# A decoder block with 64 experts: routing loops written out and reordered, and experts with three buffers for gathered rows and for down weights

## The reference, cut to what matters

```python
merged = jax.nn.sigmoid(gate_c) * y_conv + jax.nn.sigmoid(gate_a) * y_attn
h = h + merged @ w_out[l]                                  # (2064, 1024) @ (1024, 1024)
hn = rmsnorm(h, norm2_g[l])
g_logits = hn @ w_group + b_group                          # 8 groups
g_w, g_idx = max and argmax of softmax(g_logits)
e_logits = (hn @ w_router + b_router)[:, g_idx]            # 8 experts of the chosen group
top_l, top_i = lax.top_k(e_logits, 2)
w = softmax(top_l) * g_w
# each token goes to two of the 64 experts:
hb = jax.nn.silu(xb @ w_gate[e]) * (xb @ w_up[e])          # 1024 -> 256
y = hb @ w_down[e]                                         # 256 -> 1024
h = h + segment_sum(w * y)                                 # then the 16 meta tokens are dropped
```

## Time and profile before

| | |
|---|---|
| time, median of 3 runs | 2815.13 us (2812.27 to 2816.78) |
| the profiled execution's own time, and its span | 2826.66 us, 2825.0 us |
| busy in the span: PE, PEld, DVE, ACT, POOL | 89%, 71%, 62%, 37%, 20% |
| DMA | 477.69 MB, mean 169 GB/s |
| routing, 1690 to 1998 us | PE busy 233.41 of 308 us, granted clock 0.88, DMA share 0.41 |
| start of the experts, 1998 to 2042 us | PE busy 25.70 of 44 us, clock 0.70, DMA share 0.39 |
| jobs in full flow, 2042 to 2715 us | PE busy 626.23 of 673 us, clock 0.99, DMA share 0.90 at 344 GB/s |
| last jobs, 2715 to 2825 us | PE busy 77.75 of 110 us, clock 0.88, DMA share 0.52 |

### The profile page before, as it was taken

The page is one execution under the profiler, slowest core; times in us unless marked ns, Lnnn a source line. Parts: engine busy times, 40 slices in busy tenths (PEclk is TensorE's granted clock), DMA queues, the critical chain, the costliest instruction groups (busy, mean ns, idle before and its releaser), DMA issues. The chain is left out here.

```text
span 2825.0 us, 36971 instructions
## 1 busy us (share of the span) xinstructions
PE 2515.1 (89%) x12303; PEld 2017.3 (71%) x12303; DVE 1755.8 (62%) x2528; ACT 1048.6 (37%) x1524; POOL 566.6 (20%) x502
## 2 busy tenths in 40 slices
PE   4999999999899899999929998886499989999986
PEld 3898888999878798898916776665366666666652
DVE  6599997776120288888835554555466666666641
ACT  4201001443221287787821113222344444444430
POOL 3132222111111011111110010021323333333321
PEclk9999999999999999999969998998699999999998
DMA  5121212233214424345057646334388989899983
GB/s 128 46 67 54 74 52 83 75 113 113 87 65 132 125 81 107 92 126 147 16 150 198 181 142 233 122 134 164 112 342 338 351 333 354 339 342 345 351 314 136
DMA packets 181933, 477.69 MB, mean 169 GB/s; under 512 B 33292, under 2 KB 104076, under 8 KB 147372
## 3 DMA queue, kind: packets, MB, share of 16 engines
q1 hardware_dynamic: 132658, 370.45, 39.0%
q0 software_dynamic: 33264, 58.98, 6.2%
q10 hardware_dynamic: 15890, 46.67, 4.3%
HBM read 415.40 MB, written 117.21 MB: 189 GB/s over the span
## 5 line engine op out<-in xcount | busy, mean ns | idle before, releaser
L92 PE MATMUL project_bank<-project_xnT_hi,project_w_hi 128*128 128x512 f32 (+4 forms) x1352 | 511.2, 378 | 1.3 <-DVE project_xnT_lo L667 0.7
L93 PE MATMUL project_bank<-project_xnT_lo,project_w_hi 128*128 128x512 f32 (+4 forms) x1352 | 498.9, 369 | 0.0
L94 PE MATMUL project_bank<-project_xnT_hi,project_w_lo 128*128 128x512 f32 (+4 forms) x1352 | 496.7, 367 | 0.0
L717 DVE SCALAR_TENSOR_TENSOR project_work<-project_work,project_taps 128x2048 f32<-128x2048 f32 x128 | 335.5, 2621 | 4.5
L2404 DVE TENSOR_TENSOR experts_gu_lo<-weights_gate_up,experts_gu_hi 128x2048 fp32r<-128x2048 f32 x128 | 288.0, 2289 | 62.3 <-ACT experts_gu_hi L2346 61.9
L2346 ACT ACTIVATE experts_gu_hi<-weights_gate_up 128x2048 fp32r<-128x2048 f32 x128 | 244.3, 1911 | 163.7 <-DMA weights_gate_up<-in_w_up_dram 136.6
L2308 PE MATMUL experts_y_bank<-weights_down,experts_hT 128*128 128x512 f32 x544 | 256.9, 616 | 27.3 <-issue 26.3
L92 PEld LDWEIGHTS project_bank<-project_xnT_hi,project_w_hi 128*128 128x128 f32 (+1 forms) x1352 | 251.4, 186 | 36.9 <-issue 8.5
L93 PEld LDWEIGHTS project_bank<-project_xnT_lo,project_w_hi 128*128 128x128 f32 (+1 forms) x1352 | 251.2, 186 | 33.2 <-issue 6.8
L94 PEld LDWEIGHTS project_bank<-project_xnT_hi,project_w_lo 128*128 128x128 f32 (+1 forms) x1352 | 251.5, 186 | 27.2 <-issue 0.6
L1088 DVE TENSOR_TENSOR attend_pT<-attend_t_bank,attend_pT 128x512 fp32r<-128x512 f32 (+3 forms) x352 | 214.2, 615 | 23.7 <-ACT attend_pT L1038 22.7
(11 more groups left out here) (264 smaller groups left out, 4482.9 us busy)
## 6 DMA issues: line engine op xcount, KB each, us to landing
weights_gate_up<-in_w_gate_dram SPq DMA_DIRECT2D x68, 1024.0 KB
weights_gate_up<-in_w_up_dram SPq DMA_DIRECT2D x68, 1024.0 KB
weights_down<-in_w_down_dram SPq DMA_DIRECT2D x68, 1024.0 KB
project_w_raw<-in_w_in_dram SPq DMA_DIRECT2D x36, 512.0 KB, 4.1
qk_d<-project_work SPq DMA_DIRECT2D x16, 1032.0 KB, 5.4
gate_d<-project_work ACTq DMA_DIRECT2D x16, 1024.0 KB, 4.2
merge_gates<-gate_d SPq DMA_DIRECT2D x16, 1024.0 KB, 5.5
first_half<-qk_d SPq DMA_DIRECT2D x24, 512.0 KB, 15.7
```

What stands on the lines that cost most here:

```text
L92: pe.matmul(out, lhs[0], rhs[0], start=first, stop=False)
L93: pe.matmul(out, lhs[0], rhs[1], start=False, stop=False)
L94: return pe.matmul(out, lhs[1], rhs[0], start=False, stop=last)
L717: nc.vector.scalar_tensor_tensor(out=work[:, 2, 0:SEQ], in0=work[:, 1, META - 1 + q:META - 1 + q + SEQ], scalar=taps[:, bass.ds(ct, 1), q] ...
```

## The change

- **Routing.** All loops are written out. The conversion of the merged tile (c, 3) to high and low parts no longer stands in tile (c, 2) but in the tail of the chunk before, on ACT ahead of the two Exp and on DVE inside `choose` behind its eighth step (except in chunk 0). The last tile is turned into a free half of `h_bank` (`turned`) and its turn no longer waits for `lower` of the tile before. In the last chunk the logits are made in two groups of 256 tokens, the first ahead of the last turn; the former first step of `find_slots` is `take_ranks`, and for chunk 2 it runs in the last tile, the rest of `find_slots(2)` behind the last `lower`. The scatters of an expert choice k = 0 start as soon as its slots are there. The jobs are stored by two DMAs in place of four.
- **Experts.** Down weights have three rooms (`room_of`, `uses_of_room`), gathered rows and their indices three buffers (`room`, `times_loaded`, `freed`): `load_down(n)` waits for the down product of job n-3, and rows are gathered three jobs ahead. The third down room is taken from the stage's own memory. The order of the instructions in a step is as before.
- **The start of the experts.** DVE zeroes the three row buffers in place of POOL; POOL zeroes `sofar` behind the first three gathers; SP waits for job 0's rows before it loads the weights of jobs 2 and 3.
- **The first jobs** and SP's loads for them are written out on every engine; the further jobs keep their loops.

The core of the diff (left out: declarations and plain renamings of call arguments):

```diff
@@ -1563,24 +1563,22 @@
-def over_chunks(eng, tile, tail, after):
-    for j in range(CHUNK):
-        tile(0, j)
-        if j:
-            after(0, j - 1)
-    def chunk(c):
+def turned(n):
+    return t_bank if n < NT - 1 else h_bank[:, n % 2 ^ 1]
+def over_chunks(tile, tail, after):
+    for c in range(NC):
...
             tile(c, j)
-            tail(c - 1, j, False)
+            if c:
+                tail(c - 1, j, False)
...
                 after(c, j - 1)
-            tail(c - 1, j, True)
-    with eng.Fori(1, NC - 1) as c:
-        chunk(c)
-    chunk(NC - 1)
+            if c:
+                tail(c - 1, j, True)
@@ -1649,9 +1646,9 @@
 def scatter(c):
-    wait(pool, slots_ready, c * 4 + 4)
-    for j in range(CHUNK):
-        for k in range(2):
+    for k in range(2):
+        wait(pool, slots_ready, c * 4 + (3 + k))
+        for j in range(CHUNK):
@@ -1670,9 +1667,10 @@
 pe.wait_ge(hn_ready, n + 1)
-pe.wait_ge(hn_lo_ready, n + 1)
+if n < NT - 1:
+    pe.wait_ge(hn_lo_ready, n + 1)
 for i in range(DC):
-    m = nc.tensor.transpose(t_bank[:, i // 4, (i % 4) * P:(i % 4 + 1) * P],
+    m = nc.tensor.transpose(turned(n)[:, i // 4, (i % 4) * P:(i % 4 + 1) * P],
@@ -1691,16 +1689,24 @@
+def logits(c, first, end):
+    pe.wait_ge(hn_lo_ready, c * CHUNK + (end + 1))
+    pe.wait_ge(w_ready, DC + 1)
+    cols = slice(first * P, end * P)
+    for i in range(DC):
+        m = pair_matmuls(nc.tensor, r_bank[0:R, cols], (r_hi[:, i, :], r_lo[:, i, :]),
+                         (hnT_hi[:, i, cols], hnT_lo[:, i, cols]), i == 0, i == DC - 1)
+    return m
 def tail(c, part, behind):
+    last = c == NC - 1
     if part == 0 and not behind:
+        if last:
+            pe.wait_ge(slot_step, (c - 1) * 5 + 1)
+            logits(c, 0, CHUNK // 2)
...
     elif part == 1 and not behind:
-        pe.wait_ge(hn_lo_ready, c * CHUNK + (CHUNK + 1))
-        pe.wait_ge(w_ready, DC + 1)
-        for i in range(DC):
-            m = pair_matmuls(nc.tensor, r_bank[0:R, :], (r_hi[:, i, :], r_lo[:, i, :]),
-                             (hnT_hi[:, i, :], hnT_lo[:, i, :]), i == 0, i == DC - 1)
-        m.then_inc(logits_done, 1)
+        logits(c, CHUNK // 2 if last else 0, CHUNK).then_inc(logits_done, 1)
@@ -1773,18 +1780,18 @@
     elif part == 1:
+        if c < NC - 1:
+            high_m(c + 1, CHUNK - 1)
...
-over_chunks(act, tile, tail, high)
+over_chunks(tile, tail, high)
...
 act.dma_start(jobs_d[:, 0:1], job_count[:, :]).then_inc(final_stored, 16)
-for k in range(3):
-    act.dma_start(jobs_d[:, 1 + MORE_JOBS * k:1 + MORE_JOBS * (k + 1)].rearrange("o j -> j o"),
-                  job[:, k:k + 1], allow_slow_non_contiguous=True).then_inc(final_stored, 16)
-wait(act, final_stored, 64)
+act.dma_start(jobs_d[:, 1:1 + 3 * MORE_JOBS].rearrange("o (j k) -> (o j) k", k=3),
+              job[:, 0:3], allow_slow_non_contiguous=True).then_inc(final_stored, 16)
+wait(act, final_stored, 32)
@@ -1811,22 +1818,25 @@
 nc.vector.tensor_tensor(hnT_lo[:, :, j * P:(j + 1) * P],
-                        t_bank[:, :, :].rearrange("p b (c t) -> p (b c) t", t=P),
+                        turned(n)[:, :, :].rearrange("p b (c t) -> p (b c) t", t=P),
...
 s = stat[:, b, :]
-if j < CHUNK - 1:
+if j == CHUNK - 1:
+    if c < NC - 1:
+        low_m(c + 1, 0)
+elif j < CHUNK - 2 or c == 0:
     low_m(c, j + 1)
-elif not (isinstance(c, int) and c == NC - 1):
-    low_m(c + 1, 0)
...
                         x_sb[:, b, :], ALU.add).then_inc(h_ready, 1)
+if n == NT - 1:
+    take_ranks(NC - 2)
@@ -1885,6 +1895,8 @@
 step(v.tensor_reduce(e(2), p64.rearrange("p t (g j) -> p t j g", j=PER_GROUP), AX.X, ALU.add))
+if c < NC - 1:
+    low_m(c + 1, CHUNK - 1)
@@ -1915,12 +1927,14 @@
+def take_ranks(c):
+    wait(dve, rank_done, c + 1)
+    nc.vector.scalar_tensor_tensor(out=place[:, :, :].rearrange("p t n -> p (t n)"),
+                           in0=r_bank[:, 0:CHUNK * EXPERTS], scalar=float(EXPERTS),
+                           in1=index64_tiled[:, :], op0=ALU.mult, op1=ALU.add).then_inc(slot_step, 1)
...
     v = nc.vector
-    wait(dve, rank_done, c + 1)
-    v.scalar_tensor_tensor(out=place[:, :, :].rearrange("p t n -> p (t n)"),
-                           in0=r_bank[:, 0:CHUNK * EXPERTS], scalar=float(EXPERTS),
-                           in1=index64_tiled[:, :], op0=ALU.mult, op1=ALU.add).then_inc(slot_step, 1)
@@ -1938,16 +1952,19 @@
         lower(c, CHUNK - 1)
+        if c == NC - 1:
+            find_slots(c - 1)
...
         choose(c)
-    elif part == 3 and behind:
+    elif part == 3 and behind and c != NC - 2:
+        take_ranks(c)
...
 wait(dve, tiled, CHUNK)
-over_chunks(dve, tile, tail, lower)
+over_chunks(tile, tail, lower)
@@ -1983,6 +2000,16 @@
+def room_of(n):
+    return (n + 1) % 3
+def uses_of_room(n):
+    return sum(room_of(m) == room_of(n) for m in range(n + 1))
@@ -1993,8 +2020,10 @@
+self.down_rooms = {1: self.down[:, 0, :, :], 2: self.down[:, 1, :, :]}
 self.gate_up_loaded = [ctx.enter_context(nc.semaphore(f"weights_gate_up_loaded{b}")) for b in range(2)]
-self.down_loaded = [ctx.enter_context(nc.semaphore(f"weights_down_loaded{b}")) for b in range(2)]
+self.down_loaded = [ctx.enter_context(nc.semaphore(f"weights_down_loaded{b}")) for b in range(3)]
@@ -2082,15 +2113,25 @@
-def over_first_jobs(eng, step):
-    for n in range(4):
-        step(n, n % 2, n // 2, min(n, 3), 2)
-    with eng.Fori(2, EXPERTS // 2 - 1) as q:
-        for b in range(2):
-            step(q * 2 + b, b, q, 3, 2)
-    step(EXPERTS - 2, 0, EXPERTS // 2 - 1, 3, 1)
+def over_first_jobs(step):
+    for n in range(EXPERTS - 1):
+        step(n, n % 2, n // 2, min(n, 3), min(EXPERTS - 1 - n, 3))
+def room(n, b):
+    return room_of(n) if isinstance(n, int) and n < EXPERTS else b
+def times_loaded(n, b, q):
+    if isinstance(n, int) and n < EXPERTS:
+        return uses_of_room(n)
+    return q + (uses_of_room(EXPERTS - 2 + b) + 1 - EXPERTS // 2)
+def freed(n):
+    return n if isinstance(n, int) and n < EXPERTS else n + 1
@@ -2143,16 +2184,17 @@
 def load_down(n, b, e):
-    wait(sp, down_done, n + 1)
-    weights.load_down(sp, b, e)
+    wait(sp, down_done, freed(n))
+    weights.load_down(sp, room(n, b), e)
+wait(sp, rows_loaded[room_of(0)], 16)
...
 def load_list(j):
-    first = sp.value_load(job_sb[0:1, bass.ds(j + (1 + MORE_JOBS), 1)], min_val=0, max_val=SEQ - P)
-    n = sp.value_load(job_sb[0:1, bass.ds(j + (1 + 2 * MORE_JOBS), 1)], min_val=0, max_val=EXPERTS - 1)
+    first = sp.value_load(job_sb[0:1, bass.ds(j * 3 + 2, 1)], min_val=0, max_val=SEQ - P)
+    n = sp.value_load(job_sb[0:1, bass.ds(j * 3 + 3, 1)], min_val=0, max_val=EXPERTS - 1)
@@ -2164,17 +2206,13 @@
 load_down(2, 0, expert_of(2))
-for n in range(4, GROUPS):
+for n in range(4, EXPERTS):
...
     load_down(n - 1, 1 - n % 2, expert_of(n - 1))
-with sp.Fori(1, PER_GROUP) as j:
-    for g in range(GROUPS):
-        load_gate_up(j * GROUPS + g, g % 2, j + g * PER_GROUP)
-        load_down(j * GROUPS + (g - 1), 1 - g % 2, j + ((g - 1) * PER_GROUP if g else EXPERTS - PER_GROUP - 1))
-load_down(EXPERTS - 1, 1, EXPERTS - 1)
+load_down(EXPERTS - 1, 1, expert_of(EXPERTS - 1))
 def further(n, b, q):
-    j = n - EXPERTS + 1
+    j = (n - EXPERTS) * 3 + 1
@@ -2191,17 +2229,14 @@
-chain(nc.gpsimd.memset(rows[:, :, :], 0.0), 3)
-chain(nc.gpsimd.memset(sofar[:, :, :], 0.0), 4)
-pool.sem_inc(y_free, 2)
 def gather(n, b):
+    r = room(n, b)
     wait(pool, index_ready, n + 1)
-    wait(pool, x_turned, n + 1)
+    wait(pool, x_turned, freed(n))
     pool.indirect_dma_start(
-        out=rows[:, b, :], out_offset=None, in_=hn_d,
-        in_offset=bass.IndirectOffsetOnAxis(ap=from_row[:, b:b + 1], axis=0),
-        bounds_check=SEQ - 1, oob_is_err=False).then_inc(rows_loaded[b], 16)
+        out=rows[:, r, :], out_offset=None, in_=hn_d,
+        in_offset=bass.IndirectOffsetOnAxis(ap=from_row[:, r:r + 1], axis=0),
+        bounds_check=SEQ - 1, oob_is_err=False).then_inc(rows_loaded[r], 16)
@@ -2225,8 +2260,8 @@
 def step(n, b, q, before, after):
-    if after == 2:
-        gather(n + 2, b)
+    if after == 3:
+        gather(n + 3, 1 - b)
@@ -2234,9 +2269,13 @@
+wait(pool, rows_zeroed, 1)
...
 gather(1, 1)
-over_first_jobs(pool, step)
+gather(2, 0)
+chain(nc.gpsimd.memset(sofar[:, :, :], 0.0), 3)
+pool.sem_inc(y_free, 2)
+over_first_jobs(step)
@@ -2260,12 +2299,13 @@
 pe.sem_inc(hidden_turned, 2)
-pe.wait_ge(consts_ready, 4)
+pe.wait_ge(consts_ready, 2)
 def turn_rows(n, b, q):
-    pe.wait_ge(rows_loaded[b], q * 16 + 16)
+    r = room(n, b)
+    pe.wait_ge(rows_loaded[r], times_loaded(n, b, q) * 16)
     pe.wait_ge(x_lo_ready, n + 1)
-    by_chunk = rows[:, b, :].rearrange("t (p c) -> t c p", c=DC)
+    by_chunk = rows[:, r, :].rearrange("t (p c) -> t c p", c=DC)
@@ -2299,13 +2339,14 @@
 def down(n, b, q):
-    pe.wait_ge(down_loaded[b], q * 16 + 16)
+    r = room(n, b)
+    pe.wait_ge(down_loaded[r], times_loaded(n, b, q) * 16)
...
         for c in range(HC):
```

(8 more changed lines are left out.)

43 lines of the change are left out of this document (23 added, 20 removed).

## The result

| | before | after |
|---|---|---|
| time, median | 2813.7 us (4 runs, 2811.84 to 2816.78) | 2769.65 us (4 runs, 2767.03 to 2777.05) |
| ratio, 95% interval | | 0.9847 [0.9824, 0.9869], 37 to 50 us less |
| profiled execution, its span | 2826.66 us, 2825.0 us | 2767.81 us, 2766.2 us |

Faster, and 4.65 us above the predicted 2765 us.

A forecast was written before the change was run, and what follows sets the result against it. The prediction took PE with holes to bound the routing and DMA transfers the experts' jobs. Terms of 17 + 8.4 + 6.3 + 19 made 51 us; 50 off the median of 2815.13 gave 2765 us, range 2736 to 2796.

The forecast's parts named there:

- routing, chunks: Routing, chunks 1 to 3: PE's waits for m_lo and the slow clock go, 17 us, ends 10 and 21.
- routing, end: End of the routing: logits in two groups 7.3 us, scatters sooner about 1.1 us; together 8.4 us, ends 5 and 10.
- start of the experts: Start of the experts: first rows land at about 2007.4 in place of 2013.7, 6.3 us, ends 3 and 8.
- the jobs: First jobs of the experts: DMA sets the pace, 10.9 us per job in place of 11.22, 19 us over 60 jobs.
- jobs 61 to 66: Last jobs of the experts in the ledger; the prediction gave no separate term for them.
- Holes and the slow clock: Routing: PE waited 14.6 us for m_lo, and the lower clock cost 3.4 us per chunk, twice; together 21 us at most.
- The rival that I gave 0.18: Experts: DMA engines of the first partitions are already full; only holes behind late rows go, 8 us, 2775 us; chance 0.18.
- Its sign: Experts: if ACT's up-weight wait stays 2.5 us per job and DMA 0.90, the half-full engines rival holds.
- ceiling of 355 GB/s: Experts: the DMA rate of a stretch without a hole, taken as limit; gives 10.9 us per job.
- The base: Profiled execution 2826.66 us, median 11.5 us lower, perhaps lacking holes; 50 us taken off the median.
- Starving at six microseconds per fetch: Experts: PE starves for code over 19 fetches, would end at 2860 us at six; slower, chance 0.10.
- Code: Experts: rival that code fetches of written-out loops take time on a full DMA engine, 20 to 30 us back; chance 0.12.

The follow-up runs named there:

- e0: The kernel before, run and profiled once more with no edit; 2814.08 us (1 run).
- e9: The changed kernel with the merged tile (c, 3) converted in tile (c, 2) again, as before the change; 2769.91 us, ratio 0.9832 to before.
- e1: The changed routing with the experts of the kernel before; 2786.56 us, ratio 0.989 to before.
- e2: The changed experts with the routing of the kernel before; 2798.91 us, ratio 0.9933 to before.
- e10: The changed kernel without SP's wait for the rows of job 0; 2777.21 us, ratio 0.9842 to before.
- e8: The changed kernel with the lists of odd jobs shifted 64 partitions, so rows use both halves; 2752.95 us, ratio 0.9768 to before.
- e6: The changed kernel with an unused transfer of 256 KB more in each of 60 jobs, into partitions 64 to 127; 2848.08 us, ratio 1.0102 to before.
- e7: The changed kernel with an unused transfer of 256 KB more in each of 60 jobs, into partitions 0 to 63; 2938.32 us, ratio 1.0422 to before.
- e3: The kernel before with only the first jobs of the experts and SP's loads for them written out; 2813.76 us, ratio 0.9996 to before.
- e4: The changed kernel with down weights loaded one down product later, as with two rooms; 2775.49 us, ratio 0.984 to before.
- e5: The changed kernel with rows gathered two jobs ahead in place of three; 2775.03 us, ratio 0.9843 to before.
- e11: The kernel with rows in both halves of the partitions, plus down weights one product later and rows two jobs ahead; 2756.93 us, ratio 0.9782 to before.

## Why the prediction was right, and which step was not

Term by term, measured from e0 to the changed kernel on the same places of the trace:

| term | predicted | measured |
|---|---|---|
| routing, chunks | 17 | 23.3 (sums h, 223.2 to 199.9) |
| routing, end | 8.4 | 7.7 (last sum h to last scatter, 44.7 to 37.0) |
| start of the experts | 6.3 | 8.3 (last scatter to first turn, 24.0 to 15.7) |
| the jobs | 19 | 4.1 (61 jobs, 677.8 to 673.7) |
| jobs 61 to 66 | 0 | 1.8 (81.1 to 79.3) |
| sum | 51 | 45.2, of 46.3 between the two executions |

The rest lies in three stretches that no term covers: 0.8 us ahead of the first sum, 1.5 behind the last down product's start, and 1.2 the other way between the first turn and the first down product (19.0 to 20.1).

**Routing, chunks.** Holes and the slow clock went, as said, and a little more than the 21 us that I held for the upper end. But I gave the credit to the moved conversion. In e9 it has 3.5 us, and the loops written out have the rest; that the shorter `choose` is what does it is read from the timeline and was not run by itself. I had named its 4.4 us and not counted them in the sum. That `choose` ends sooner is the same as m_lo not being late, and I had both rows in hand.

**Routing, end.** Right within a microsecond, the second group of logits at the distance predicted. Its length was not: half of 8.2 us was to be 4.1, and it took 5.4 at the lower clock, where the whole ran at 0.68 on average (1957.5 to 1965.8 us of the kernel before).

**Start.** Right in sum, with the parts moved. From the first memset to the first turn 14.6 us became 9.2, 5.4 us in place of 6.3. The other 2.9 us lie ahead of the memset, where the prediction put the two stores of the jobs in place of four at nothing; e1 and e2 bear out that it goes with them or with the new start of the experts, and don't part the two. SP's wait, which I took as part of the gain, gives no time by itself (e10). What counts is that the first gather is issued 5.1 us ahead of the weights, where it was 1.5 us before.

**The jobs: the step that failed** is "What then sets the pace is the DMA. At a job's 3.87 MB, the 355 GB/s of a stretch without a hole give 10.9 us". The DMA does set the pace, but not as one rate for the core. The term has 19 us in the prediction and 4.1 in the ledger (14.7 against the slower profile that it was read from). The rival that I gave 0.18 is the one that the runs bear out in the main: the lists fill from partition 0, and what serves the first half of the partitions carries weights and rows, the rest weights. It said 8 us and 2775 us, a pace of 11.09 us; the pace after is 11.04. Its sign was in my forecast too: ACT's wait for up weights is not shorter, the DMA share is 0.91.

The row that I held against it, 0.98 busy for ten microseconds, says little: of the 60 windows of ten microseconds from 2100 to 2700 us of the kernel before, 6 reach 0.97. Single microseconds say more. Of the 500 from 2100 to 2600 us the changed kernel has 318 at 0.95 or more and 53 from 0.45 to 0.60, about half of the engines; e8 has 344 and 31. e6 and e7 (72 and 162 us for the same bytes) and e8 (22 us for the same bytes moved elsewhere) are what shows that the place counts. Whether the engines are full or what lies behind them at the partitions, the runs don't tell, since e7's transfer was spread over sixteen parts and still cost most.

The Trainium skill, *DMA: Bandwidth & Descriptors*, The descriptor swizzle, gives a mapping for a transfer to 128 partitions, engines 0 to 7 to partitions 0 to 63. The loads of e9, which land as eight parts and then eight, agree with such a split; they don't name single engines. The extra transfers of e6 and e7 fill 64 partitions, and that mapping is not stated for them.

I also had rows against a ceiling of 355 GB/s, and didn't use them. One is another of those six windows. The other is from the time when the first gather of the kernel before was under way, with mainly loads of weights beside it (94.1% of 16 engines' time, the gather 6.5%):

```profile
2280.00:2290.00 10.00, 7.33 (x30) 4.56 (x29) 6.30 (x8) 3.99 (x4) 2.60 (x4) 1.00 1.02 393
...
2007.20:2011.20 4.00, 0.00 (x0) 0.00 (x0) 0.00 (x0) 0.00 (x0) 0.23 (x1) 0.50 1.01 422
```

393 GB/s over ten microseconds, and 422 GB/s from DRAM to SBUF over four. The limit of about 358 GB/s between HBM and SBUF, which the same page of the Trainium skill states (Where 436 GB/s comes from), is half of what it gives a stack of two cores. With one core at work here it is no ceiling; the measurement decides.

**The base.** That the profiled execution of before held holes that the median has not was right, and was most of its 12 us. Yet I still counted those holes once among the 19 us of the jobs and took all of 50 us off the median. The total came out within 5 us because the routing gave 6 more, the start and the last jobs 4 more and the jobs 15 less. That the errors nearly cancel is luck, and no confirmation of the pace.

**A slip in a rival.** Starving at six microseconds per fetch would not end at 2860 us: 2815 + 19 x 6 - 51 is 2878, and 2860 is the value for five. No chance hung on it.

**Code.** It costs nothing that can be measured in the experts (e3), and in the routing writing out was the larger gain.

## What to carry to other kernels

Read the DMA share as a mean over engines. Here 0.90 busy with work queued meant that some were full while others were not, and deeper buffers mostly moved the wait from one name to another (e4, e5, e11). Look at which partitions the partly filled transfers use: placing every second one in the other half cost two more table loads and gave 22 us, half of what the whole change had given. Where a loop's engine is late for its neighbour, count the small steps of the late engine in a loop and out of it: `choose` took 4.5 us less written out, and a chunk with its loops written out 10 us less.

## What the runs showed of the hardware that was not expected

- 256 KB more per job in partitions 64 to 127 cost 1.2 us per job, in partitions 0 to 63 2.7 us. Both are more than the rival or the theory gave, and the second is more than its bytes explain at the 208 GB/s of the fuller half (0.262 MB takes 1.26 us). In its trace one part of sixteen of each down load lands 9 us behind the others; why it is one part stays open.
- DVE's chain of dependent steps of 4 to 288 columns took 14.6 us in a loop and 10.1 us written out, with the same durations of the single steps: 0.45 us for the copy, 0.16 for the last product. The difference lies between the steps.
- Transfers of weights with one gather beside them ran at 422 GB/s for four microseconds (kernel before); weights and gathered rows in full flow at 380 GB/s for sixty with the engines 0.97 busy (e8).
